# A hybrid decoder layer on one core: the first gate/up tile woven into the last output projections, and a new order of small operations at two stage switches

## The reference

```python
u = rms_norm(h, norm1_gain);  proj = u @ w_in
o_rec = hgrn2_mixer(...)       # gated linear recurrence, 4 heads of 128
o_att = swa_sink_mixer(...)    # sliding-window attention with sinks, 8 heads of 64
h = h + concat(o_rec, o_att) @ w_out
u = rms_norm(h, norm2_gain)
h = h + (silu(u @ w_gate) * (u @ w_up)) @ w_down      # d_ff = 2816
```

## Time and profile before

| | |
|---|---|
| median of 3 runs | 1215.82 us (1212.56 to 1218.23) |
| profiled execution, its own time | 1217.93 us |
| its span, first to last instruction | 1216.2 us |
| mean granted TensorE clock | 0.978 |
| PE busy | 1159.8 us, 95% of the span |
| DVE, ACT, POOL busy | 710.3, 503.0, 462.7 us |
| from 620 us to 970 us | PE busy 100% of the time |

### The profile page before, as it was taken

The page is one execution under the profiler, slowest core; times in us unless marked ns, Lnnn a source line. Parts: engine busy times, 40 slices in busy tenths (PEclk is TensorE's granted clock), DMA queues, the critical chain, the costliest instruction groups (busy, mean ns, idle before and its releaser), DMA issues.

```text
span 1216.2 us, 14507 instructions
## 1 busy us (share of the span) xinstructions
PE 1159.8 (95%) x5472; PEld 947.3 (78%) x5472; DVE 710.3 (58%) x863; ACT 503.0 (41%) x772; POOL 462.7 (38%) x355
## 2 busy tenths in 40 slices
PE   4999999999999999979699999999999989999998
PEld 4998776668888878856588888888888867888876
DVE  7305566658768886577833333233332376787785
ACT  6314445553545451245433333333333344544541
POOL 6301113334525141040354544545445363433452
PEclk9999989999999999989799999999999999999999
DMA  6101100000110501230133223332233385454433
GB/s 243 52 1 36 53 18 1 18 26 27 36 35 1 191 14 62 82 139 0 52 113 113 90 93 113 113 113 84 99 113 113 118 308 196 130 173 131 155 109 143
DMA packets 37094, 112.63 MB, mean 93 GB/s; under 512 B 4897, under 2 KB 9761, under 8 KB 35617
## 3 DMA queue, kind: packets, MB, share of 16 engines
q1 hardware_dynamic: 37024, 111.71, 26.9%
HBM read 83.12 MB, written 28.57 MB: 92 GB/s over the span
## 4 chain that ended last, share of the span: by engine, by line
PE 82%; DVE 7%; ACT 4%; issue 3%; POOL 3%; DMA 1%; SPq 0%; DVEq 0%; ACTq 0%; POOLq 0%
PE ps L1205 24%; PE ps L1206 23%; PE ps L1207 23%; PE ps L1382 4%; PE ps L1343 1%; PE ps L1357 1%; PE ps L1358 1%; DVE ulo L1585 1%; DVE olo L1816 1%; PE ps L1221 1%; POOL D L698 1%; DVE vlo L1579 1%; DMA ubraw<-hidden 1%; DMA araw<-wd 1%; DVE B L1710 1%
## 5 line engine op out<-in xcount | busy, mean ns | idle before, releaser
L1205 PE MATMUL ps<-ubhi,adhi 128*128 128x512 f32 x308 | 122.2, 397 | 8.2 <-DVE yacc L1889 6.2
L1206 PE MATMUL ps<-ublo,adhi 128*128 128x512 f32 x308 | 121.5, 394 | 0.0
L1205 PE MATMUL ps<-uhi,whi 128*128 128x512 f32 x272 | 113.2, 416 | 0.0
L1557 DVE TENSOR_TENSOR glo<-graw,ghi 128x1024 fp32r<-128x1024 f32 x21 | 26.8, 1276 | 147.3 <-POOL s34raw L613 147.3
L1207 PE MATMUL ps<-uhi,wlo 128*128 128x512 f32 x272 | 107.3, 394 | 0.0
L1206 PE MATMUL ps<-ulo,whi 128*128 128x512 f32 x272 | 107.1, 394 | 0.0
L698 POOL TENSOR_TENSOR D<-B 128x1024 f32<-128x1024 f32 x28 | 63.6, 2270 | 44.8 <-DVE M L1743 23.8
L711 POOL TENSOR_TENSOR hst<-sg,up 128x512 f32<-128x512 f32 x21 | 27.9, 1327 | 136.8 <-DMA hidden<-hst 70.3
L1205 PEld LDWEIGHTS ps<-ubhi,adhi 128*128 128x128 f32 x308 | 58.8, 191 | 23.3 <-DVE yacc L1889 7.6
L1205 PE MATMUL ps<-ohi,s34hi 128*128 128x512 f32 x168 | 66.8, 398 | 10.6 <-ACT ps L1041 10.6
L1889 DVE TENSOR_TENSOR yacc<-ps,yacc 128x512 f32<-128x512 f32 x104 | 69.2, 685 | 12.2 <-PE ps L1207 12.1
(11 more groups left out here) (283 smaller groups left out, 3123.7 us busy)
## 6 DMA issues: line engine op xcount, KB each, us to landing
hidden<-hst SPq DMA_DIRECT2D x11, 1792.0 KB, 8.5
ubraw<-hidden SPq DMA_DIRECT2D x33, 512.0 KB, 5.2
graw<-wg SPq DMA_DIRECT2D x21, 512.0 KB, 4.2
uraw<-wu SPq DMA_DIRECT2D x21, 512.0 KB, 3.4
wraw<-wproj SPq DMA_DIRECT2D x17, 512.0 KB, 3.5
araw<-wd SPq DMA_DIRECT2D x22, 384.0 KB, 4.3
x<-xT SPq DMA_DIRECT2D x8, 512.0 KB, 6.8
h<-xT SPq DMA_DIRECT2D x8, 512.0 KB, 4.5
```

Of the source, the lines that this page charges most:

```text
L1205: nc.tensor.matmul(out, whi_, xhi_, start=first, stop=False, skip_group_check=seeded)
L1206: nc.tensor.matmul(out, whi_, xlo_, start=False, stop=False, skip_group_check=seeded)
L1557: nc.vector.tensor_tensor(glo[g % 2][:, :], graw[g % 2][:, :], ghi[g % 2][:, :].bitcast(F32), ALU.subtract)\
```

## The change

Five edits, all in the order of the work, none in the arithmetic:

1. In `schedule()`, after O 39: `norm_sum(0)` and `norm_rstd(0)`, three output groups, and then steps k = 0 to 7 of the first gate/up tile ("FG"), with output groups 43 to 47 behind k = 0 to 4, and `norm_sum(1)` behind k = 6. Each engine follows that order. `norm_rstd(1)` now stands behind the whole tile half.
2. `norm_sum` waits for each of its inputs by itself.
3. From the end of tile 0 on: on ACT, `gate_hi(2)` and `seed_c(1)` go ahead of the operand made from `t4`; on DVE, `hid_2_first` and `gate_lo(2)` go ahead of `t4`, and `hid_1(0)` goes behind `up_2(1)`; POOL's `weight_sums(2)` waits for `t4`.
4. At the switch to the down projection: the weights of stage 1 are loaded with those of stage 0, POOL's sums of both are made earlier, and ACT and DVE put the PSUM copies and adds (`down_seed_b(0)`, `down_add`) ahead of hi and lo parts. For this, buffers get other addresses and semaphores.
5. Hidden unit 2 is loaded before the third residual tile.

```diff
-    order += [("O", 40 + g, 0) for g in range(8)] + [("XS", 1)]
+    order += [("XS", 1), ("SS", 0)]
+    order += [("O", 40 + g, 0) for g in range(3)]
+    for k in range(KT):
+        order += [("FG", 0, k)] + ([("O", 43 + k, 0)] if k < 5 else [("SS", 1)] if k == 6 else [])
...
@@ ACT
+                elif kind == "SS" and step[1] == 0:
+                    norm_rstd(0)
+                elif kind == "FG":
+                    k = step[2]
+                    act.wait_ge(s_un, k + 1)
+                    if k == 0:
+                        act.wait_ge(s_omm, 32)
+                    operand_hi(k // 4, k % 4, k % 4 + 1, h[:, 0, k, :])
...
-            for k in range(KT):
-                act.wait_ge(s_un, k + 1)
-                if k == 0:
-                    act.wait_ge(s_omm, 32)
-                operand_hi(k // 4, k % 4, k % 4 + 1, h[:, 0, k, :])
-                if k == 2:
-                    norm_rstd(1)
+            norm_rstd(1)
             gate_hi(1)
...
+            gate_hi(2)
+            seed_c(1)
             for c in range(2):
                 act.wait_ge(s_t4, c + 1)
                 operand_hi(3, 2 * c, 2 * c + 2, h[:, 0, 4 + 2 * c:6 + 2 * c, :])
-            seed_c(1)
             a22_hi(1)
-            gate_hi(2)
+            silu_1(1)
             s12_hi(2)
-            silu_1(1)
             silu_2(1)
...
                 silu_1(g)
+                if g == LAST:
+                    weight_hi(1, 0)
+                    sums_hi(1, 0)
                 silu_2(g)
-            weight_hi(1, 0)
+            down_seed_b(0)
             weight_hi(1, 1)
-            down_seed_b(0)
             unit_hi(1, 0)
             down_seed_c(0)
+            sums_hi(1, 1)
             unit_hi(1, 1)
-            sums_hi(1, 0)
             down_seed_b(1)
             unit_hi(1, 2)
             down_seed_c(1)
-            sums_hi(1, 1)
             unit_hi(1, 3)
...
@@ PE
             def norm_sum(x):
-                pe.wait_ge(s_nsq, 8 * x + 8)
-                pe.wait_ge(s_nacc, 3 * x + 3)
-                for m in (0, 2, 4, 6, 7):
+                for i, m in enumerate((0, 2, 4, 6, 7)):
+                    pe.wait_ge(*((s_nacc, 3 * x + i + 1) if i < 3 else (s_nsq, 8 * x + m + 1)))
...
-                    if g == 45:
-                        norm_sum(0)
+                elif kind == "SS":
+                    norm_sum(step[1])
+                elif kind == "FG":
+                    if step[2] == 0:
+                        pe.wait_ge(s_w0lo, 2)
+                    first_group(0, step[2])
...
@@ DVE
+                elif kind == "FG":
+                    k = step[2]
+                    if k == 0:
+                        norm_tile(0, 0)
+                    if k + 1 < KT:
+                        norm_tile(0, k + 1)
+                    operand_lo(k // 4, k % 4, k % 4 + 1, h[:, 0, k, :], k + 1)
...
+            hid_2_first()
+            gate_lo(2)
             for c in range(2):
                 kk = slice(2 * c, 2 * c + 2)
                 dve.wait_ge(s_t2, c + 1)
...
-            hid_1(0)
-            hid_2_first()
             a22_lo(1)
-            gate_lo(2)
             gate_2(1)
             up_2(1)
+            hid_1(0)
             s12_lo(2)
...
             weight_lo(1, 0)
+            sums_lo(1, 0)
+            hid_1(LAST)
             weight_lo(1, 1)
-            hid_1(LAST)
             keep_e(0)
-            unit_lo(1, 0)
             down_add("C11", 0)
-            unit_lo(1, 1)
             down_add("C12", 0)
             down_add("C22", 0)
-            sums_lo(1, 0)
+            unit_lo(1, 0)
             keep_e(1)
+            sums_lo(1, 1)
             down_add("C21", 0)
+            unit_lo(1, 1)
+            down_add("C11", 1)
             unit_lo(1, 2)
-            down_add("C11", 1)
-            sums_lo(1, 1)
             down_add("C12", 1)
...
@@ POOL
+            pool.wait_ge(s_t4, 2)
             weight_sums(2)
             hidden_sums(0)
             for g in range(1, GROUPS):
                 if 2 <= g < LAST:
                     weight_sums(g + 1)
                 if g == LAST:
-                    down_sums(0)
                     down_sums(1)
                 hidden_2(g)
                 hidden_sums(g)
+                if g == LAST - 1:
+                    down_sums(0)
...
@@ SP
                 if g == LAST - 1:
                     sp.wait_ge(s_prod, done[2, g])
-                    weights_in(0, 0, 3)
-                    weights_in(0, 3, 4)
+                    for s in range(2):
+                        weights_in(s, 0, 3)
+                        weights_in(s, 3, 4)
...
-            sp.wait_ge(s_prod, done[6, LAST])
-            weights_in(1, 0, 3)
-            weights_in(1, 3, 4)
...
-            for q in range(3):
-                residual_in(q)
+            residual_in(0)
+            residual_in(1)
+            for i in range(4):
+                unit_in(2, i)
+            residual_in(2)
```

More of the change, by code:

```diff
@@ L370, in build @@
         s_ohi, s_olo = sem("operand_hi"), sem("operand_lo")
-        s_graw = [sem(f"gate_or_down_w{i}_in") for i in range(2)]
-        s_uraw = [sem(f"up_or_down_w{i}_a22_in") for i in range(2)]
+        s_graw = [sem(f"gate_w{i}_in") for i in range(2)]
+        s_uraw = [sem(f"up_w{i}_in") for i in range(2)]
         s_sum = sem("weight_sums")
@@ L381, in build @@
         s_yin = s_x[4:8]
[L382 to L383 removed]
+        s_a3 = s_w0
+        s_a1 = s_wraw
         s_ub = [s_vraw[0:4], s_vraw[4:8], s_x[0:4]]
@@ L558, in _ @@
                 n = 2 * s - 3
-                unit = s < STAGES - 1
+                unit = 3 <= s < STAGES - 1
                 if unit:
@@ L842, in norm_rstd, with operand_hi @@
                 nc.scalar.activation(nrs[:, x, :], nrs[:, x, :], ACT.Exp, scale=-0.5).then_inc(s_nrs, 1)
+            def operand_hi(i, c0, c1, src):
+                nc.scalar.activation(ohi[i][:, c0:c1, :], src, ACT.Copy).then_inc(s_ohi, 1)
             for g in range(V_FIRST + 1):
@@ L1217, in norm_sum, with first_group @@
             def norm_sum(x):
-                pe.wait_ge(s_nsq, 8 * x + 8)
-                pe.wait_ge(s_nacc, 3 * x + 3)
-                for m in (0, 2, 4, 6, 7):
+                for i, m in enumerate((0, 2, 4, 6, 7)):
+                    pe.wait_ge(*((s_nacc, 3 * x + i + 1) if i < 3 else (s_nsq, 8 * x + m + 1)))
                     mm = nc.tensor.matmul(ps[:, 4 + x, :], ones[:, :], nsq[x][m][:, :], start=m == 0, stop=m == 7)
                 mm.then_inc(s_nss, 1)
+            def first_group(half, k):
+                a, b, c, e = banks(0)
+                w = slice(k * P, (k + 1) * P)
+                if half == 0:
+                    pe.wait_ge(s_olo, k + 1)
+                    hi, lo = ohi[k // 4][:, k % 4, :], olo[k // 4][:, k % 4, :]
+                elif k < 4:
+                    pe.wait_ge(s_b12lo, k + 1)
+                    hi, lo = b12hi[:, k, :], b12lo[:, k, :]
+                else:
+                    pe.wait_ge(s_olo, 8 + k - 3)
+                    hi, lo = ohi[2][:, k - 4, :], olo[2][:, k - 4, :]
+                mg = three(ps[:, (a, c)[half], :], g0hi[:, w], g0lo[:, w], hi, lo, k == 0, k == KT - 1)
+                mu = three(ps[:, (b, e)[half], :], u0hi[:, w], u0lo[:, w], hi, lo, k == 0, k == KT - 1)
+                if k == KT - 1:
+                    mg.then_inc(s_first, 1)
+                    mu.then_inc(s_first, 1)
             pe.wait_ge(s_pool0, 2)
@@ L1470, in product @@
                     product_part(p, g, k)
-            def first_group(half):
-                a, b, c, e = banks(0)
-                for k in range(KT):
-                    w = slice(k * P, (k + 1) * P)
-                    if half == 0:
-                        pe.wait_ge(s_olo, k + 1)
-                        hi, lo = ohi[k // 4][:, k % 4, :], olo[k // 4][:, k % 4, :]
-                    elif k < 4:
-                        pe.wait_ge(s_b12lo, k + 1)
-                        hi, lo = b12hi[:, k, :], b12lo[:, k, :]
-                    else:
-                        pe.wait_ge(s_olo, 8 + k - 3)
-                        hi, lo = ohi[2][:, k - 4, :], olo[2][:, k - 4, :]
-                    mg = three(ps[:, (a, c)[half], :], g0hi[:, w], g0lo[:, w], hi, lo, k == 0, k == KT - 1)
-                    mu = three(ps[:, (b, e)[half], :], u0hi[:, w], u0lo[:, w], hi, lo, k == 0, k == KT - 1)
-                    if half == 0 and k == 1:
-                        norm_sum(1)
-                mg.then_inc(s_first, 1)
-                mu.then_inc(s_first, 1)
             def down_product(p, n):
@@ L1528, in down_product @@
                 mm.then_inc(s_dprod, 1)
-            pe.wait_ge(s_w0lo, 2)
-            first_group(0)
-            first_group(1)
+            for k in range(KT):
+                first_group(1, k)
             for p, g in products[:-1]:
@@ L1898, in keep_e @@
                     nc.vector.tensor_tensor(p5acc[q][:, :], ps[:, e, :], p5acc[q][:, :], ALU.add).then_inc(s_dadd, 1)
-            norm_tile(0, 0)
```

(4 more changed lines are left out.)

64 lines of the change are left out of this document (33 added, 31 removed).

## The result

| | before | after |
|---|---|---|
| median of 4 runs each | 1215.55 us (1212.56 to 1218.23) | 1236.82 us (1233.01 to 1238.25) |
| ratio, 95% interval | | 1.0171 (1.0137 to 1.0205) |
| profiled execution, its own time | 1217.93 us | 1233.01 us |
| its span; mean granted clock | 1216.2 us; 0.978 | 1231.3 us; 0.976 |

The kernel is slower, by 21.3 us. The forecast was 1224, and the measured time is above the range of 1210 to 1232. The profiled execution of after is the shortest of its four, so the traces differ by 15.1 us only.

What follows compares the result with a forecast made beforehand. PE was taken to bound the kernel, busy 95% of the span. The terms 23.5 - 5.3 - 9.9 = +8.3 us gave 1226 for the profiled execution, 1224 as the median, range 1210 to 1232.

Steps and rivals of the forecast that it cites:

- A: The interleaved first gate/up tile, up to its half 1: claimed to cost 23.5 us, bounds 17 and 29.
- The five waits for a lo part: PE's waits on DVE between O 42 and FG 5, one per round: some 2.5 to 3 us each.
- The rounds: Five rounds of FG k and O 43+k in the first tile, serial through ACT's and DVE's queues: 31.9 us together.
- The sign that failed: Forecast sign in the first tile's five rounds: a granted clock near 0.75.
- B: End of tile 0, bank copy put ahead of the operand from `t4`: claimed to give 5.3 us (4.5 to 10.3).
- The first idle time: PE idle before product 3 of tile 1, behind ACT's `gate_hi(2)` and `seed_c(1)`: 1.9 us.
- The new wait before product 4: PE waiting for DVE's `up_2(1)`, late through DVE colliding with POOL's `weight_sums(2)`: 3.3 us.
- C: The switch to the down projection: claimed to give 9.9 us (6 to 11.5).
- the two old waits: PE's waits at the down-projection switch: 5.0 us cut to about 1, and 1.9 us for an ACT copy gone.
- The rounds overlap: Rival: later hi parts aren't held by squares, a round takes 2.05 us, the kernel 1203 us; chance 0.12.
- Serial rounds at the full clock: Rival: the first tile's rounds stay serial but run at full clock, +1 to +3, 1218 us; chance 0.20.
- The repairs fall short: Rival: DVE-POOL collisions throughout B or late stage 2 weights at C; B 3, C 6, 1230 us; chance 0.13.

Runs made afterwards that it cites:

- e3: The changed kernel with ACT's hi part and DVE's lo part of the next tile put ahead of the square and the add: 1217.65 us, ratio 1.0017.
- e5: The changed kernel with only ACT's hi part of the next tile put ahead of the square, DVE's order as in the change: 1229.94 us (one run).
- e2: The kernel before with edits 3 to 5 alone, the first tile's list order as before: 1207.99 us, ratio 0.9930.
- e7: e2 with stage 1's loads behind the store of unit 9, and unit 10's store ahead of residual tiles 2 and 3: 1203.04 us, ratio 0.9905.
- e10: e7 with ACT's PSUM copies and DVE's adds of output 3 put ahead of stage 2's weight hi and lo parts: 1206.06 us (one run).
- e4: The changed kernel with the loads of stage 1's weights issued behind the store of hidden unit 9: 1234.44 us, ratio 1.0146.
- e8: e3 with two more output groups ahead of FG 0, the rest behind k = 0 to 2, and POOL's `weight_sums(1)` behind its pair sums: 1206.27 us, ratio 0.9927.
- e11: e8 with the orders of e7 and e10: 1201.15 us, ratio 0.9891.
- e6: e2 with POOL's `weight_sums(2)` held back until DVE's two lo parts of `t4` are written: 1209.46 us (one run).
- e9: The kernel before with edits 4 and 5 alone: 1216.47 us, ratio 1.0010.
- e1: The kernel before with edits 1 and 2 alone: 1242.02 us, ratio 1.0209.

## Why the prediction was right in its direction and wrong in its size

**A: right in mechanism, 3.4 us low.** Forecast 23.5, with bounds of 17 and 29; measured 26.9 and 27.7. FG 0 was to start at 542.2. It starts at 539.40, which is 542.1 on before's clock (the first row of the table puts after 2.7 us ahead). The wait for POOL's sums was to be 4 to 5 us and is 4.70. The five waits for a lo part were to be 2.5 to 3 us and are 2.69 to 3.34. The rounds take 33.6 us and not 31.9: I took 6.9 us for the first and 5.9 for each other one, with 1.4 for collisions; the rows give 7.5, then 6.9, 6.5, 6.9 and 5.7; PE came back at the lower clock, or fell to it within the round. FG 5, FG 6 and `norm_sum(1)` had 7.7 us, with 1.0 of it for the lower clock, and took 9.5 (572.96 to 582.48), since FG 5 and 6 ran at the lower clock throughout, 5.3 us where 2.8 were counted. That is 1.7 + 1.8 us, less 0.1 up to FG 0. The sign that failed is the clock: near 0.75 was forecast for the rounds, from the earlier trace rows, and it was 0.60. e3 and e5 show the chain.

**B: right, 2 us low.** Forecast 5.3 (4.5 to 10.3), measured 7.3 in the traces of after, e2, e7 and e10, and 8.2 in those of e4, e5, e8 and e11, where product 4 runs at the full clock (12 matmuls in 3.5 us and not 4.4). The first idle time is 1.71 us (1.9 forecast). The new wait before product 4 came too, at 1.93 us and not 3.3: I gave the pair of lo parts the 4.55 us of the earlier trace rows, and it took 3.46, so that DVE reached `up` 9.6 us behind the start of product 3 (612.63 to 622.19) and not 11.6 (588.2 to 599.8). The forecast left out the 0.67 us of `up` itself, which made its wait 0.7 us too short. e6 shows both the collision and that without it the wait goes elsewhere.

**C: the step that failed.** Forecast -9.9 us (bounds 6 and 11.5), measured -2.1 in the trace of after, -1.4 in e9's, +1.7 in e2's, and a ratio of 1.001. What the prediction said of the two old waits did happen: the 5.0 us wait is gone, and n = 1 to 2 is 7.1 us shorter. Wrong was "the DMA issues moved ahead (...) put residual tile 2 some 5 us later, and it isn't due before 1003", as the only price of the moved loads, with stage 2's weights at 0.9 us, and that the moved sums cost nothing ("POOL was idle there, and ACT is in wait for PE"). Behind the change PE waits 8.9 us at this switch, where the sum had 2.1. Three things were left out:

1. The four weight loads stand on SP ahead of the store of unit 9, and POOL, ACT and a PSUM copy hang on that store: product 3 of tile 21 comes 1.7 to 2.5 us later than before the change in the traces with that order. e4 and e7 move the store ahead and win 2.0 and 2.5 us there.
2. POOL's sums of stage 1 now run beside all of DVE's four lo parts of unit 0. These take 6.26 us (5.27 before), and `up` of tile 21 is late by 0.7, with 1.0 us on PE. This is read from the traces; no run isolates it.
3. PE gets to n = 2 some 7 us sooner, but the transfers don't. The DMA engines of after, 1000 to 1036 us in 40 slices, tenths busy:

```profile
DMA  9999200389999999999999999999978966204770
```

   They are busy for 90% or more of the time from 1008 to 1026 us, and for 70% or more up to 1029. The store of unit 10, issued at 1017.34, lands 11.6 us later, and POOL gets stage 2's weights at 1031.32 after a wait of 14.0 us. That is 12.4 us behind the start of n = 2; before it was 5.5 us (1011.51, against 1006.03). So PE waits again, 1.9 and 1.8 us and 1.1 for an add, and n = 2 to 4 takes 23.9 to 27.5 us in all traces with this switch but e11's, beside 22.2 and 20.5 without it (before, e1). I had taken 0.9 us for it, with 1.5 as the bound, though the earlier trace rows show a DMA share of 0.88.

Part of C's spread from trace to trace is luck with the clock. In n = 2 to 4 it is 1.00 in after, e1, e5, e9 and e11, and 0.87 to 0.94 in the other traces, that of before too. At 1.00 the stretch takes 23.9 to 24.5 us with the switch of the change (after, e9) and 20.5 without (e1): 3.5 to 4.1 us dearer. From product 1 of tile 21 to n = 4 it then takes 59.1 and 59.8 us, beside 59.9 in e1, so that C is worth nearly nothing, as e9's time says. Why the clock differs with the same code isn't shown.

What stays open is how much of point 3 can be mended: e7 and e10 took little of it, e11 brought 21.97 us, and its copies, adds and loads are those of e10. Only what runs before differs. Of the 3.4 us, 1.6 are the clock, and the rest is PE's shorter wait behind a load that came 1.3 us sooner; with one trace of each, I can't say whether either comes from the new first tile.

**The rivals.** "The rounds overlap" didn't occur, and e3 shows what it would have needed. "Serial rounds at the full clock" fell: the clock was 0.60 in them. "The repairs fall short" (B 3, C 6) named the right side, and late weights of stage 2 as the cause, but put B too low and C too high. By the measured terms the sum is 26.9 - 7.3 - 2.1 = +17.5 us, where I had +8.3: A's cost was put 3.4 too low, C's gain 7.8 too high and B's gain 2.0 too low. The other 3.8 us of the medians' +21.3 lie in executions that have no trace, and their place isn't shown.

## What to carry to other kernels

When work of two chains is woven on PE, write down for each in-order queue what stands between one tile's parts and the next tile's: if both ACT and DVE have an operation of the other chain there, each round costs the whole chain (6.7 us for 2.05 us of matmuls), and issuing the operands one tile ahead on both queues takes it away (19 us here). Price a moved load by what stands behind it on the issuing queue, stores above all, and follow who waits for these. When a stall is removed in front of a stretch in which the DMA engines are busy nearly all of the time, count on its return: 7.1 us were won, and of these 3.5 to 4.1 were paid back in the next two outputs at the same clock, and 2.8 ahead of it, with the late store and the slower lo parts.

## What was not expected of the hardware

- With gaps of 2.7 to 3.3 us, one in each round of 6.7 us, the granted clock was 0.60 over 33.6 us. With gaps of under 0.9 us (e3) it was 0.50 for the first 5.3 us behind FG 0, 0.99 over the next 10.5 and 1.00 after that.
- Issuing is not free: six loads took SP 2.98 us, some 0.5 us each. In e7 the four loads right behind the store of unit 9 took 4.43 us (from 953.40), the last three of them 1.3 us each.
- A store of 1.75 MB (1792 KB) let POOL go on 9.0 us after its issue at 962.13. One of the same size landed 11.6 us after its issue at 1017.34, behind 4 MB of residual tiles and 1.75 MB of hidden values.
- The same code took 22.21 and 20.45 us in n = 2 to 4 (before, e1), at a granted clock of 0.92 and 1.00.
